# One loop over eight pairs of heads instead of two stages of four

## The reference

```python
def mixer_odd(h, pos, row, col, w_in, cq_norm, w_cq_up, ckv_norm, w_ckv_up, dq_norm, dk_norm, w_out):
    proj = h @ w_in
    ...
    cq = (rmsnorm(cq, cq_norm) @ w_cq_up).reshape(b, s, C_HEADS, C_NOPE + C_ROPE)
    q_nope, q_rope = cq[..., :C_NOPE], rope(cq[..., C_NOPE:], pos, ROPE_THETA)
    kv = (rmsnorm(ckv, ckv_norm) @ w_ckv_up).reshape(b, s, C_HEADS, C_NOPE + C_V)
    k_nope, v_c = kv[..., :C_NOPE], kv[..., C_NOPE:]
    k_rope = rope(ck_rope, pos, ROPE_THETA)
    ...
    c_out = block_attention(q_c, k_c, v_c)
    dq = axial_rope(rmsnorm(dq.reshape(b, s, D_KV_HEADS, D_GROUP, HEAD_DIM), dq_norm), row, col)
    dk = axial_rope(rmsnorm(dk.reshape(b, s, D_KV_HEADS, HEAD_DIM), dk_norm), row, col)
    d_out = block_attention(dq, dk, dv)
    return jnp.concatenate([c_out, d_out], axis=-1) @ w_out
```

## Time and profile before

| | |
|---|---|
| median of three runs | 4160.29 us |
| the profiled execution | 4163.94 us |
| its span | 4162.0 us |
| TensorE busy | 3667.5 us (88% of the span) |
| VectorE busy | 2459.1 us (59%) |
| ScalarE busy | 1639.2 us (39%) |
| mean granted TensorE clock | 0.942 of full speed |

### The profile page before, as it was taken

How to read it: one execution, slowest core, us unless ns; L and a number is a source line. 1 busy time by engine, 2 the same in 40 slices (tenths; PEclk the granted TensorE clock), 3 DMA queues, 4 the chain that set the end, 5 groups by cost and what they waited for, 6 DMA issues and landing times. The chain is left out here.

```text
span 4162.0 us, 58111 instructions
## 1 busy us (share of the span) xinstructions
PE 3667.5 (88%) x23128; PEld 3009.1 (72%) x23128; DVE 2459.1 (59%) x3919; ACT 1639.2 (39%) x2307; POOL 333.0 (8%) x195
## 2 busy tenths in 40 slices
PE   6988999978989999998898997699786998994996
PEld 4767777867778888886797776477685776773774
DVE  3466771568765565657233654777663666637786
ACT  5223432168320000003112753366533666623775
POOL 0011111000000000000000000233100000000441
PEclk9989999989999999999999998799898999996998
DMA  5011223530522111112124223599624103043998
GB/s 193 17 49 45 77 71 142 190 139 27 183 108 84 40 52 49 40 60 86 66 74 130 69 101 136 201 368 364 219 76 129 37 7 130 16 148 119 372 365 291
DMA packets 193759, 527.57 MB, mean 127 GB/s; under 512 B 27448, under 2 KB 126568, under 8 KB 174464
## 3 DMA queue, kind: packets, MB, share of 16 engines
q1 hardware_dynamic: 177216, 467.21, 30.5%
q0 software_dynamic: 13200, 55.17, 4.6%
q10 hardware_dynamic: 3120, 2.10, 0.2%
HBM read 433.05 MB, written 91.37 MB: 126 GB/s over the span
## 5 line engine op out<-in xcount | busy, mean ns | idle before, releaser
L2484 ACT ACTIVATE mlp_relu<-mlp_z 128x512 f32<-128x512 f32 x64 | 38.3, 598 | 616.2 <-PE mlp_z L168 616.2
L3668 DVE TENSOR_TENSOR ring_r<-ring,oN_r 128x4096 fp32r<-128x4096 f32 x48 | 212.4, 4424 | 72.7 <-ACT oN_r L3574 72.7
L166 PE MATMUL scans_G<-ring_r 128*128 128x512 f32 x544 | 221.8, 408 | 32.3 <-ACT scans_stg L3034 18.3
L3668 DVE TENSOR_TENSOR ring_r<-ring,hT_r 128x4096 fp32r<-128x4096 f32 x48 | 212.3, 4422 | 54.6 <-ACT hT_r L3574 53.2
L3574 ACT ACTIVATE oN_r<-ring 128x4096 fp32r<-128x4096 f32 x48 | 174.1, 3630 | 80.2 <-DMA ring<-in_w_all 78.5
L166 PE MATMUL mlp_z<-oN_r,mlp_w_high_r 128*128 128x512 f32 x512 | 200.3, 391 | 5.6 <-DVE ring_r L2525 5.6
L3574 ACT ACTIVATE hT_r<-ring 128x4096 fp32r<-128x4096 f32 x48 | 174.1, 3631 | 68.0 <-DMA ring<-in_w_all 67.9
L167 PE MATMUL mlp_z<-hT_r,mlp_w_high_r 128*128 128x512 f32 x512 | 200.0, 391 | 0.0
L168 PE MATMUL mlp_z<-oN_r,ring_r 128*128 128x512 f32 x512 | 199.9, 390 | 0.0
L166 PE MATMUL mlp_y_ps<-mlp_w_high_r,ring_r 128*128 128x512 f32 x512 | 199.7, 390 | 0.0
L167 PE MATMUL mlp_y_ps<-ring_r 128*128 128x512 f32 x512 | 199.3, 389 | 0.0
(11 more groups left out here) (685 smaller groups left out, 10201.5 us busy)
## 6 DMA issues: line engine op xcount, KB each, us to landing
ring<-in_w_all SPq DMA_DIRECT2D x110, 2048.0 KB, 19.6
ring<-in_w_mlp SPq DMA_DIRECT2D x16, 2048.0 KB, 8.4
ring<-in_w_all SPq DMA_DIRECT2D x12, 1024.0 KB, 6.2
branch_gates<-scans_stg SPq DMA_DIRECT2D x48, 256.0 KB, 2.0
merge_raw<-branch_gates SPq DMA_DIRECT2D x16, 768.0 KB, 5.0
diff_gemm_more<-in_w_all POOLq DMA_DIRECT2D x10, 1024.0 KB, 7.1
oN<-x_rows SPq DMA_DIRECT2D x16, 512.0 KB, 8.9
ring<-in_w_all POOLq DMA_DIRECT2D x6, 1024.0 KB, 6.0
```

The source lines that it names most:

```text
L166: pe.matmul(out, lh, rh, start=start, stop=False)
L2484: act.activation(r[:, n % 2, :], Z[:, n % 4, :], ACT.Relu).then_inc(z_free, 1)
L3668: dve.tensor_tensor(buf_r[:, b, :], buf[:, b, :], w_high[n % RING].bitcast(F32), ALU.subtract)\
```

## The change

The two heads stages become one, with a loop of eight pairs: pairs 0 to 3 are the grouped ones, 4 to 7 the latent ones. The buffers for queries and keys are allocated ahead of `mla_gemm` and live through both stages; the weight ring is used for them no more. The scores, the turned exponentials and the values lie in `oN`, which is free by then. The grouped pair 0 is loaded at the start of `mla_gemm`, cast by ScalarE at the end of that stage's step 3 and subtracted by VectorE at the end of step 4; the heads stage starts with its scores. The first latent pair, which is 3584 columns wide as it brings the rotated key with it, is loaded, cast and subtracted inside the loop like the others. The ring is fed behind the loads of pair 5. The results go to the same rows of `hT`.

```diff
-def mla_gemm_stage(nc, m, slot):
+def load_grouped(m, sp, qk, pair, sem):
+    for what, of in ((0, 16 + 3 * (pair // 2) + pair % 2), (1, 16 + 3 * (pair // 2) + 2)):
+        sp.dma_start(qk[:, pair % 2, what * S:(what + 1) * S], m["qkT"][of, :, :]).then_inc(sem, 16)
+def mla_gemm_stage(nc, m, slot, qk, qk_low, qk_high):
...
+        PAIR_AT, BOTH = 3, slice(0, 2 * S)
...
             sp.dma_start(sin[:], m["sin_mla"]).then_inc(par_in, 16)
+            load_grouped(m, sp, qk, 0, pair_in)
...
+                if n == PAIR_AT:
+                    act.wait_ge(pair_in, 32)
+                    act.activation(qk_high[:, 0, BOTH], qk[:, 0, BOTH], ACT.Copy).then_inc(pair_cast, 1)
...
+                if n == PAIR_AT + 1:
+                    dve.wait_ge(pair_cast, 1)
+                    dve.tensor_tensor(qk_low[:, 0, BOTH], qk[:, 0, BOTH], qk_high[:, 0, BOTH].bitcast(F32), ALU.subtract)\
+                       .then_inc(pair_split, 1)
+            dve.wait_ge(pair_split, 1)
...
-        PAIRS, K0 = 4, 0 if mla else 4
+        GROUPED, PAIRS = 4, 8
...
-        v = st.sb("v", [P, 2, NT, VW])
-        sc = st.sb("sc", [P, 3, S])
-        pT = st.sb("pT", [P, 3, NT, P])
+        lent = m["oN"][:, :, :].rearrange("p t d -> p (t d)")
+        sc = lent[:, 0:3 * S].rearrange("p (b s) -> p b s", b=3)
+        pT = lent[:, 3 * S:6 * S].rearrange("p (b k n) -> p b k n", b=3, n=P)
+        v = lent[:, 6 * S:8 * S].rearrange("p (b k n) -> p b k n", b=2, n=P)
...
+        LOADS = [0, 2, 2, 2, 6, 6, 6, 6]
+        WIDTH = [2 * S] * GROUPED + [QK_W] + [3 * S] * 3
...
-                if p == 1 and not mla:
+                if p == GROUPED + 1:
                     m["ring"].feed(sp)
...
-                if n == -1 or (n % NT == 5 and n // NT + 1 < PAIRS):
+                if n >= 0 and n % NT == 5 and n // NT + 1 < PAIRS:
...
-        heads_stage(nc, m, "mla")
-        m["ring"].limit = m["ring"].total
-        heads_stage(nc, m, "gqa")
+            mla_gemm_stage(nc, m, slot, qk, qk_low, qk_high)
+            m["ring"].limit = m["ring"].total
+            heads_stage(nc, m, qk, qk_low, qk_high)
```

More of the change, by code:

```diff
@@ L1123, in _, with heads_stage @@
                 dve.nop().then_inc(x_ready, 1)
-def heads_stage(nc, m, kind):
-    with Stage(nc, kind) as st:
-        mla = kind == "mla"
-        PAIRS, K0 = 4, 0 if mla else 4
-        N = PAIRS * NT
[L1133 to L1139, removed]
-        v = st.sb("v", [P, 2, NT, VW])
-        sc = st.sb("sc", [P, 3, S])
-        pT = st.sb("pT", [P, 3, NT, P])
+                if n == PAIR_AT + 1:
[3 more added lines that the diff above has]
+            dve.wait_ge(pair_split, 1)
+def heads_stage(nc, m, qk, qk_low, qk_high):
+    with Stage(nc, "heads") as st:
+        GROUPED, PAIRS = 4, 8
+        N = PAIRS * NT
+        lent = m["oN"][:, :, :].rearrange("p t d -> p (t d)")
+        sc = lent[:, 0:3 * S].rearrange("p (b s) -> p b s", b=3)
+        pT = lent[:, 3 * S:6 * S].rearrange("p (b k n) -> p b k n", b=3, n=P)
+        v = lent[:, 6 * S:8 * S].rearrange("p (b k n) -> p b k n", b=2, n=P)
         table = st.sb("table", [P, S])
@@ L1155, in heads_stage, with latent, loaded @@
         v_in = [st.sem(f"v_in{b}") for b in range(2)]
[L1156 to L1159, removed]
+        kr_in = st.sem("kr_in")
+        QR, KR = slice(2 * S, 3 * S), slice(3 * S, QK_W)
+        LOADS = [0, 2, 2, 2, 6, 6, 6, 6]
+        WIDTH = [2 * S] * GROUPED + [QK_W] + [3 * S] * 3
+        def latent(p):
+            return p >= GROUPED
+        def loaded(p):
+            return 16 * sum(LOADS[p % 2:p + 1:2])
         def pair_of(t_, p):
-            if not mla:
-                return t_[:, p % 2, :, :]
-            return t_[:, p % 2, 0:KR.stop if p == 0 else QR.stop]
+            return t_[:, p % 2, 0:WIDTH[p]]
         block = st.block()
@@ L1173, in _ @@
                     sp.wait_ge(scored, 2 * NT * (p - 1))
-                if mla:
-                    g, j = divmod(p, 2)
+                if latent(p):
+                    g, j = divmod(p - GROUPED, 2)
                     for a in range(2):
@@ L1182, in _ @@
                               .then_inc(qk_in[b], 16)
[L1183 removed]
+                            if p == GROUPED:
                                 sp.dma_start(qk[r:r + 32, 0, KR], m["qkT"][10, 0:32, half * HALF:(half + 1) * HALF])\
                                   .then_inc(kr_in, 16)
[L1186 to L1188 removed]
+                elif p:
+                    load_grouped(m, sp, qk, p, qk_in[b])
                 if p >= 2:
                     sp.wait_ge(pv_done, NT * (p - 1))
[L1191 to L1192 removed]
+                c, width = (P * (p - GROUPED), P) if latent(p) else (HALF + 64 * (p // 2), 64)
+                sp.dma_start(v[:, b, :, 0:width], m["v"][:, c:c + width].rearrange("(t p) c -> p t c", p=P))\
                   .then_inc(v_in[b], 16)
[L1194 removed]
+                if p == GROUPED + 1:
                     m["ring"].feed(sp)
@@ L1202, in _ @@
                     b = p % 2
-                    if qb == 0:
-                        pe.wait_ge(low, p + 1)
+                    mla = latent(p)
+                    if qb == 0 and p:
+                        pe.wait_ge(low, p)
                     if n >= 0:
@@ L1259, in _ @@
                         for hd in range(2):
-                            vv = v[:, b, kb, :] if kind == "gqa" else v[:, b, kb, 64 * hd:64 * hd + 64]
+                            vv = v[:, b, kb, 64 * hd:64 * hd + 64] if latent(w // NT) else v[:, b, kb, 0:64]
                             ins = pe.matmul(OR[64 * hd:64 * hd + 64, g % 2, o:o + P], vv, pT[:, (2 * w + hd) % 3, kb, :],
@@ L1319, in shift @@
                     dve.wait_ge(t_done, 2 * (u - 3) + 2)
+                scale = 96.0 ** -0.5 if latent(u // (2 * NT)) else 0.125
                 dve.memset(wait_taker[:, u % 4:u % 4 + 1], 0.0)
```

22 lines of the change are left out of this document (12 added, 10 removed).

## The result

The changed kernel takes 4122.47 us (median of 4 runs, 4118.97 to 4125.15), against 4159.51 us for the kernel before on the same chip. The ratio is 0.9912, with a 95% interval of 0.9901 to 0.9924: 37.0 us less, between 31.6 and 41.2. Forecast were 4127.1 us and a gain of 33.2.

A forecast was written before the change was run, and what follows sets the result against it. TensorE bounds both attention loops, so the time to be had lies in the holes between and around them. Terms: 38.1 - 2.0 - 2.9 = 33.2 us gained, from 4160.29 to 4127.1 us; range 4119 to 4138.

The forecast's parts named there:

- Start of the heads stage: Heads stage start: with pair 0 ready, first scores come 0.03 us after SP's first issue; gain 18.86 us.
- Joint: Between the two kinds of pairs: one loop removes drain, barrier, load, cast, subtraction and fill; gain 18.38 us.
- only the joint: Rival, heads stage start: pair 0's scores still start late, awaiting the subtraction; gain 16.3 us, time 4144 us; chance 3%.
- One start at half clock fewer: Latent part of the loop: its first three steps no longer run slow; gain 0.85 us.
- Cast of pair 0: In `mla_gemm`, steps 3 and 4: added ScalarE and VectorE work delays TensorE; cost 2.0 us, bounds 0 and 4.2.
- Wide cast: Fourth pair of the loop: first latent pair's cast and subtraction make TensorE wait; cost 2.9 us, bounds 0.35 and 7.1.
- Loads, ring feed, table, buffers, nothing: In-loop loads, ring feed, exponential's table load and moved buffers cost nothing; the table's bound is 1.28 us.
- the lent tile `oN`: Rival, attention loop: slower access to `oN` or the new buffer costs 0.26 us a step, time 4144 us; chance 4%.
- `out_odd` and all behind it would last as long as before: Sign, stages behind the heads: unchanged lengths; a later stage giving time back would make the prediction wrong.
- The clock doesn't waver at the wide cast: Denies rival, fourth pair: the wait halves the clock for some steps, price 0.85 to 5.64 us, time 4131; chance 7%.
- The half clock doesn't stay after the start: Denies rival, attention loop: TensorE stays at 1.2 GHz; 4309 us if the whole grouped part ran so; chance 1%.
- The queues of `mla_gemm`: Rival, projection stage: 1 MB of loads ahead of its first stores costs 4.7 us, time 4132 us; chance 6%.

The follow-up runs named there:

- start only: Kernel before, still two stages of four pairs, but grouped first and pair 0 made ready in `mla_gemm`; latent stage fetches its own first pair: 4149.58 us, ratio 0.9972.
- pieces: Changed kernel with each in-loop cast and subtraction cut into pieces of 1024 columns (512 for the rotated key), one a step: 4123.09 us, ratio 0.9915 to before.
- joint only: Changed kernel, one loop of eight pairs, but pair 0 loaded, cast and subtracted in the heads stage: 4131.22 us, ratio 0.9928 to before.
- early wide cast: Changed kernel with ScalarE's 3584-column cast one step earlier in the fourth pair, VectorE's subtraction where it was: 4126.97 us, ratio 0.9921 to before.

## Why the prediction was right

The gain of the two stages was put at 33.2 us and came out at 32.7, or 33.9 by the means of three traces each. The prediction was worked out from the first trace of before, so the terms below are held against that one. By its steps:

- **Start of the heads stage, 18.86 us.** It happened as the step put it: the first scores 0.05 us behind the first DMA (0.03 in the sum). Nothing took the place of the wait; clearing of the table and the values' load ran beside the scores. As a change by itself it brings less, since then the latent stage, now second, keeps its own fetch.
- **Joint, 18.38 us.** The step goes from 5.64 to 6.54 us without a barrier or a drain. The kernel that has the joint alone confirms it from the other side. It also shows that a rival was priced wrongly: "only the joint" was put at a gain of 16.3 us, as if the hole of 18.9 us at the start stayed. With the grouped pair first that hole is 11.1, and the gain was 24.4.
- **One start at half clock fewer, 0.85 us.** The latent part, from its first scores to the mark, was put at 219.23 us and took 3599.62 - 3380.41 = 219.21. The grouped part kept a slow start and paid a little more for it: four scores from 3194.79 to 3212.72 took 17.93 us against 17.44 in the grouped stage before. That is 0.49 us which the sum didn't have, and with it the whole miss against this trace. But 0.85 is what one trace of before happened to show: in the second its latent start costs 2.04 us over three full steps (3211.07 to 3232.73), in the third 0.45 (3218.11 to 3238.18). Hitting the two stages' gain to half a microsecond is luck to that extent.
- **Cast of pair 0, 2.0 us.** `mla_gemm` is 1.97 us longer. Its sum (1.15 + 0.99, less a bit) came from the idle time ahead of what queues behind each long instruction, and TensorE's two waits for VectorE's rotation (0.82 and 0.80 us) stand where it put them. With the cast at the end 0.6 us are left.
- **Wide cast, 2.9 us.** 0.93 + 2.01 = 2.94 us. VectorE's part holds by its working: what goes beyond a grouped subtraction counts in full, 0.35 + 1.61 against 2.01. ScalarE's 0.9 met 0.93, but by luck in part: no row gave it, and one step earlier the same cast costs 0.66.
- **Loads, ring feed, table, buffers, nothing.** Both steps last as before, so the lent tile `oN` doesn't slow them. The ring was fed at 3393.00 us, and `out_odd` takes 108.1 us against 108.6. The table load took 1.28 us from 3194.75, and the first exponential waited for VectorE until 3199.14: hidden. The Trainium skill (ScalarE: Activation LUTs, What ACT_TABLE_LOAD costs) has about 2.66 us for a switch, of which some 1283 ns are the load. The load agrees with the trace; here it is covered.

The rest of the difference to the forecast, 4122.47 against 4127.1, is in the unchanged stages. The prediction gave them no term of their own. It said that `out_odd` and all behind it would last as long as before. That holds for `out_odd`. The last expert stage took 414.6 to 417.8 us in the three traces before and 413.7 to 414.1 after, which is part of the 5 us left open above.

**Rivals.** The clock doesn't waver at the wide cast in the changed kernel: it is 1.00 in all stretches around it, though TensorE waits 0.89, 1.14 and 0.59 us there. But the rival is real: with ScalarE's cast one step earlier the clock fell once behind the cast for about 3 us and cost 1.51 us, inside the 0.85 to 5.64 that its price was bounded by. The Trainium skill (TensorE: Matmul & The Clock Gate, A second HAM failure mode: psum-queue depth-cycling) tells of short pauses between groups of matmuls that make the clock swing. That one dip may be of this kind, though it comes once and in one trace of six; the loops with their waits of 0.35 and 0.51 us in every pair show none. The half clock doesn't stay after the start: from 3230 us on it is 1.00. The queues of `mla_gemm` don't pay the 4.7 us of the rival: the stage with the two loads but without the cast in its middle takes 47.8 us, at most 0.7 more than without them. And the scores of pair 0 did start at once.

## What to carry to other kernels

Where two stages run the same loop over different data, the price of their border is to be read as one interval, from where the next step of the first loop would have begun to the first step of the second; and the first operand of a loop is best made ready in the stage before, if a hole at its start is what bounds it. Work put on a helping engine costs, at its new place, at most its duration less the idle time ahead of the instruction that queues behind it. In `mla_gemm` that bound was nearly met (2.1 against 1.97 us). In the attention loop the cost was far below it (0.42 us for a subtraction of 2.28), as what queued there could come later without harm, and only what went beyond that counted in full. Cutting it up helps only in steps that have idle time for a piece: measure it for each kind of step, also for steps that look alike but where the helping engine has one more write.

## What the runs showed of the hardware

- The same ten loads were in 8.9 us after the first issue where their rows had been stored long before, and in 11.6, 13.1 and 13.4 us where the stage before had just stored them. The stage before ends only when its stores have landed, so none of them was under way. The loads also go to different buffers in the two kernels; what delays them wasn't tried.
- The slow start isn't of one length. At a granted clock of 0.50, scores take 0.80 us in place of 0.50. From the first scores of the heads stage to the third it is 12.29 us in all three traces of the changed kernel, in start only and in pieces, 11.66 to 11.77 in the three kernels with the cast at the end of `mla_gemm`, 11.41 in joint only, and 11.08 with the early wide cast, where the second scores are fast already. In the latent start of the kernel before it is 13.92, 15.14 and 13.53 us in three traces.
- The clock can fall in the middle of a full loop, for about 3 us behind two waits that add up to 1.7 us, and at nearly the same waits it doesn't. One trace of six with the whole wide cast shows it.
- Two expert stages with the same code took 796.8 to 809.0 us in thirteen traces of nine kernels. A few us of gain are to be read stage by stage: the medians of the whole program hide 4 us, or show 4 us that aren't the change's.
